# Expert routing computed from the unnormalised residual

## The reference

```python
xl = xl + g1_l[:, None] * yl
hl2 = modulate(rms_norm(xl, norm_ffn[i]), sh2_l, sc2_l)
xl = xl + g2_l[:, None] * expert_choice_ffn(hl2, router[i], w_gate[i], w_up[i], w_down[i])

def rms_norm(x, g):      # modulate(h, shift, scale) = h * (1 + scale) + shift
    return x * rsqrt(mean(x * x, axis=-1) + EPS) * g

def expert_choice_ffn(h, router, w_gate, w_up, w_down):
    cap = 2 * n // 16                       # 32 tokens for each of 16 experts
    aff = softmax(h @ router, axis=-1)
    gate, idx = top_k(aff.transpose(0, 2, 1), cap)
    xg = h[bidx, idx]
    hid = silu(xg @ w_gate) * (xg @ w_up)
    y = (hid @ w_down) * gate[..., None]
    return zeros_like(h).at[bidx, idx].add(y)
```

## Time and profile before

| | us |
|---|---|
| median of 3 runs (lowest, highest) | 1381.2 (1380.23, 1385.59) |
| profiled execution, its span | 1381.7 |
| TensorE busy | 1168.3 (85%) |
| VectorE busy | 625.0 (45%) |
| ScalarE busy | 432.9 (31%) |
| DMA | 338.65 MB, 245 GB/s mean |
| experts of layer 0: first gate matmul to last down chunk | 387.2 to 597.8 |
| experts of layer 1 | 737.5 to 937.5 |

### The profile page before, as it was taken

How to read it: one execution, slowest core, us unless ns; L and a number is a source line. 1 busy time by engine, 2 the same in 40 slices (tenths; PEclk the granted TensorE clock), 3 DMA queues, 4 the chain that set the end, 5 groups by cost and what they waited for, 6 DMA issues and landing times.

```text
span 1381.7 us, 19453 instructions
## 1 busy us (share of the span) xinstructions
PE 1168.3 (85%) x8209; PEld 864.1 (63%) x8209; DVE 625.0 (45%) x1142; ACT 432.9 (31%) x783; POOL 77.9 (6%) x118
## 2 busy tenths in 40 slices
PE   5999979999986656689999665668999999999887
PEld 2777758876832212159994221216999778899766
DVE  3655874555520101146753011015994555545574
ACT  2546523312300000044341000003545663443552
POOL 3000224430000000000000000000000000100000
PEclk9999999999998889899999898989999989999998
DMA  9745964238689999985759999997354213355000
GB/s 330 288 160 206 325 224 139 106 130 307 244 316 409 409 409 409 409 316 183 305 215 377 409 409 410 409 409 284 123 183 140 105 55 129 122 183 184 0 1 31
DMA packets 125099, 338.65 MB, mean 245 GB/s; under 512 B 8657, under 2 KB 11590, under 8 KB 125014
## 3 DMA queue, kind: packets, MB, share of 16 engines
q1 hardware_dynamic: 117536, 334.51, 63.7%
q10 hardware_dynamic: 7478, 2.91, 0.8%
HBM read 336.35 MB, written 1.05 MB: 244 GB/s over the span
## 4 chain that ended last, share of the span: by engine, by line
PE 61%; DMA 26%; DVE 8%; ACT 2%; SPq 2%; issue 1%; ACTq 0%; DVEq 0%
PE bank L684 9%; PE bank L686 9%; PE bank L685 9%; DMA arena<-in_w_up_dram 6%; DMA expert_slots<-in_w_gate_dram 5%; DMA weight_ring<-in_w_up_dram 4%; DMA weight_ring<-in_w_gate_dram 3%; DMA expert_slots<-in_w_down_dram 3%; PE bank L971 3%; PE bank L586 3%; DVE arena L1902 3%; PE bank L1144 2%; PE bank L816 2%; PE bank L663 2%; PE bank L664 2%; DMA weight_ring<-in_ada_w_dram 2%
## 5 line engine op out<-in xcount | busy, mean ns | idle before, releaser
L684 PE MATMUL bank<-input_high,weights_high 128*128 128x256 f32 (+1 forms) x992 | 290.5, 293 | 8.2 <-DVE input_low L1902 7.5
L686 PE MATMUL bank<-input_high,weights_low 128*128 128x256 f32 (+1 forms) x992 | 283.9, 286 | 0.0
L685 PE MATMUL bank<-input_low,weights_high 128*128 128x256 f32 (+1 forms) x992 | 283.8, 286 | 0.0
L1902 DVE TENSOR_TENSOR weights_low<-weight_ring,weights_high 128x1024 fp32r<-128x1024 f32 x142 | 173.6, 1224 | 165.5 <-ACT weights_high L1439 165.2
L684 PEld LDWEIGHTS bank<-input_high,weights_high 128*128 128x128 f32 x992 | 188.3, 190 | 13.7 <-issue 10.6
L1439 ACT ACTIVATE weights_high<-weight_ring 128x1024 fp32r<-128x1024 f32 x142 | 149.6, 1055 | 143.5 <-PE bank L686 143.1
L686 PEld LDWEIGHTS bank<-input_high,weights_low 128*128 128x128 f32 x992 | 188.5, 190 | 0.0
L685 PEld LDWEIGHTS bank<-input_low,weights_high 128*128 128x128 f32 x992 | 187.9, 189 | 0.7
L1902 DVE TENSOR_TENSOR arena<-arena,bank 128x512 f32<-128x512 f32 (+1 forms) x38 | 24.6, 651 | 261.2 <-PE bank L971 240.2
L971 PE MATMUL bank<-arena 128*32 128x512 f32 x384 | 61.2, 773 | 50.0 <-DMA arena<-in_w_up_dram 38.8
L971 PEld LDWEIGHTS bank<-arena 128*32 128x32 f32 x384 | 12.3, 129 | 96.7 <-DMA arena<-in_w_up_dram 43.5
(11 more groups left out here) (414 smaller groups left out, 1748.2 us busy)
## 6 DMA issues: line engine op xcount, KB each, us to landing
weight_ring<-in_ada_w_dram SPq DMA_DIRECT2D x24, 2048.0 KB, 9.4
weight_ring<-in_w_gate_dram SPq DMA_DIRECT2D x16, 2048.0 KB, 23.6
arena<-in_w_up_dram SPq DMA_DIRECT2D x16, 2048.0 KB, 24.2
weight_ring<-in_w_down_dram SPq DMA_DIRECT2D x16, 2048.0 KB, 24.0
arena<-in_w_down_dram SPq DMA_DIRECT2D x12, 2048.0 KB, 20.3
weight_ring<-in_even_w_in_dram SPq DMA_DIRECT2D x9, 2048.0 KB, 8.6
arena<-in_w_gate_dram SPq DMA_DIRECT2D x8, 2048.0 KB, 21.4
weight_ring<-in_w_up_dram SPq DMA_DIRECT2D x8, 2048.0 KB, 16.2
```

The lines of the kernel that those rows point to most:

```text
L684: pe.matmul(b[:, 0:width], hi[:, k, :], XHI[:, k, t0:t0 + width], start=k == 0, stop=False)
L685: pe.matmul(b[:, 0:width], hi[:, k, :], XLO[:, k, t0:t0 + width], start=False, stop=False)
L686: mm = pe.matmul(b[:, 0:width], lo[:, k, :], XHI[:, k, t0:t0 + width], start=False, stop=k == KD - 1)
L1902: return dve.tensor_tensor(out_, a, b, op)
```

## The change

**The routing** takes the residual as it is. For a token x with root r the logit is r * (x . (gain * router)) + shift . router, where gain = (1 + scale) * norm weight. `router_gains` (VectorE) makes `GS` (gain and shift) and `RTG` = router times gain; `route_prepare` (TensorE) sums shift . router, the same on all partitions (`BROW`), and turns `GS`. `route_behind` puts into the output product, behind quarter 0, four tiny matmuls that bring gain and shift into the order of the gathered features (`GPERM`); behind quarter 4, eight transposes of residual tiles; behind quarter 7, six more, then the products of seven tiles with `RTG` in four column groups (`LPART`), two more transposes, and the logits. ScalarE (`route`, `token_rows`) squares each transposed piece from PSUM with an accumulator and copies it to `H2`; so each token's sum of squares is on its own partition, and the root is taken of 128x2 numbers. ScalarE scales `H2` by the root beside the selection. Gain and shift are applied when the gathered tokens leave PSUM.

**The selection** reads its bank without a copy; the mask is turned apart from the running count and multiplied behind the transpose; `PT` is made first for four experts, then for twelve. The gather drains in four quarters. The norms over features of `norm(1, ...)` and `norm(3, ...)` are gone, and `h2T` is no longer written there.

**The slots** are filled in another order, and slots 8 and 9 wait for the product's input to be split instead of for the token transposes. The small DMAs of ScalarE are issued behind the scaling of `H2`. The diff, cut:

```diff
-FILL_ORDER = (4, 5, 0, 1, 2, 3, 6, 7, 8, 9)
+FILL_ORDER = (4, 5, 0, 1, 8, 9, 2, 3, 6, 7)
...
-            warm(8)
-            pe.wait_ge(vector_drained, n["v"])
...
+            def route_prepare(ly):
+
+                pe.wait_ge(route_prep, ly + 1)
+                b = v_open()
+                for k in range(KD):
+                    pe.matmul(b[:, 0:16], GS[:, 8 + k:9 + k].broadcast_to([P, P]), RT[:, k, :], start=k == 0, stop=k == KD - 1)
+                v_close(pe.transpose(b[0:16, P:2 * P], GS, ident[:, :]), ("route", ly))
...
+                    if m == 4:
+                        tokens(0, 4)
+                    if m == KD - 1:
+                        tokens(4, 3)
+                        b = v_open()
+                        for k in range(KD - 1):
+                            j = 32 * (k % 4)
+                            mm = pe.matmul(b[j:j + 32, 0:T], RTG[:, 16 * k:16 * k + 32], XH[:, k, META:L2], start=k < 4, stop=k >= 3)
+                        parts = v_close(mm, ("parts", ly))
+                        pe.wait_ge(vector_drained, mark[(name, KD - 1)])
+                        b = s_open()
+                        mm = transposes(b, [(b[:, tt * P:tt * P + P], XH[:, KD - 1, META + tt * P:META + tt * P + P]) for tt in range(TT)])
+                        s_close(mm, ("last_rows", ly))
...
+            pe.wait_ge(vector_drained, n["v"])
+            route_prepare(0)
+            warm(4)
             for j in range(2):
-                product(W_EVO + j, 4 * j, T, v_open, v_close, "out1", new_input=j == 0, after=norm_behind(1, T, SQn))
+                product(W_EVO + j, 4 * j, T, v_open, v_close, "out1", new_input=j == 0, after=route_behind(0, "out1"))
...
-                warm(9)
-                pe.wait_ge(router_in, 16 * (ly + 1))
...
-                turn_tokens(0)
+                warm(4)
                 pe.wait_ge(aff_ready, ly + 1)
...
-                turn_tokens(1)
-                warm(4)
+                warm(6)
+                pe.wait_ge(mask_ready, ly + 1)
...
-                warm(2)
-                pe.wait_ge(pick_ready, 2 * ly + 1)
-                pe.wait_ge(scalar_drained, n["s"])
+                warm(1)
+                pe.wait_ge(pick_ready, 3 * ly + 1)
+                pe.wait_ge(tokens_scaled, 4 * (ly + 1))
...
                 if slot_of(cn) >= LATE_SLOT:
-                    sp.wait_ge(scalar_filled, mark[("h2", stream[cn][1])])
+                    sp.wait_ge(input_split, KD * (1 + 2 * stream[cn][1]))
...
+            def token_rows(ly, tt, k0, count):
+
+                b = take()
+                act.activation(SQJ[:, 0:count * P], b[:, 0:count * P], ACT.Square,
+                               accum_out=tok_sum[:, k0 // 4, tt:tt + 1]).then_inc(token_squares, 1)
+                drained(act.activation(H2[:, tt, k0 * P:(k0 + count) * P], b[:, 0:count * P], ACT.Copy))
+                act.wait_ge(scalar_drained, n["s"])
...
             def experts(ly):
                 act.wait_ge(sm_args, ly + 1)
                 act.activation(AFFT, AFFT, ACT.Exp).then_inc(sm_exps, 1)
+                act.wait_ge(scalar_drained, n["s"])
+                act.wait_ge(token_rstd, ly + 1)
+                for tt in range(TT):
+                    for kh in range(2):
+                        h = H2[:, tt, 512 * kh:512 * kh + 512]
+                        act.activation(h, h, ACT.Copy, scale=tok_rstd[:, tt:tt + 1]).then_inc(tokens_scaled, 1)
...
-            norm(1, ("out1",), mod=(0, 24))
+            route(0)
...
+            def router_gains(ly):
+
+                dve.wait_ge(router_in, 16 * (ly + 1))
+                then(stt(GS[:, 0:8], MOD[:, ly, 32:40, 0], 1.0, vec("norm_ffn", 8 * ly, 8), ADD, MUL))
+                then(dve.tensor_copy(GS[:, 8:16], MOD[:, ly, 24:32, 0]))
+                tt(RTG.rearrange("p (k e) -> p k e", k=KD), RT, last(GS[:, 0:8], 16), MUL).then_inc(route_prep, 1)
...
-                drained(dve.tensor_copy(AT2[0:EXP, :], b[0:EXP, 0:T]), True)
...
-                tt(PS2[0:EXP, :], PS2[0:EXP, :], MT2[0:EXP, :], MUL).then_inc(pos_ready, 1)
-                b = take()
-                drained(dve.tensor_copy(POS, bank(b, 2, 16)), True)
+                b = take()
+                dve.wait_ge(scalar_drained, mark[("maskT", ly)])
+                drained(tt(POS, bank(b, 2, 16), MASKT, MUL), True)
...
-                for t_, pt in enumerate(pts):
-                    ins = tt(pt, last(POS[:, t_, :], CAP), mid(SLOTN, EXP), ALU.is_equal)
-                ins.then_inc(pick_ready, 1)
+                for e0, e1 in ((0, EG), (EG, EXP)):
+                    for t_, pt in enumerate(pts):
+                        ins = tt(pt[:, e0:e1, :], last(POS[:, t_, e0:e1], CAP), mid(SLOTN, e1 - e0), ALU.is_equal)
+                    ins.then_inc(pick_ready, 1)
```

More of the change, by code:

```diff
@@ L928, in experts @@
                 v_close(mm, ("affT", ly))
-                turn_tokens(1)
-                warm(4)
+                warm(6)
+                pe.wait_ge(mask_ready, ly + 1)
+                b = s_open()
+                for tt in range(TT):
+                    mm = pe.transpose(b[:, 16 * tt:16 * tt + 16], MT2[0:EXP, tt * P:tt * P + P], ident[0:EXP, 0:EXP])
+                s_close(mm, ("maskT", ly))
                 pe.wait_ge(pos_ready, ly + 1)
@@ L966, in experts @@
                             w = weights(cn + q, "p (e k n) -> p e k n", e=EG, k=2)
-                            if part == 0 and q == 2:
-                                pe.wait_ge(vector_drained, gathered)
+                            if part == 0:
+                                pe.wait_ge(*gathered[q])
                             for k in range(2):
@@ L1034, in _ @@
             product(W_SC + 5, 4, T, v_open, v_close, "gb")
-            warm(8)
+            route_prepare(1)
+            warm(4)
             for j in range(2):
-                product(W_SC + 6 + j, 4 * j, T, v_open, v_close, "out2", new_input=j == 0, after=norm_behind(3, T, SQn))
+                product(W_SC + 6 + j, 4 * j, T, v_open, v_close, "out2", new_input=j == 0, after=route_behind(1, "out2"))
             mark[("split", 1)] = len(quarters)
@@ L1670, in _, with route @@
                     drained(act.activation(OT[:, :, u * P:u * P + P], bank(b, 4, P), ACT.Copy))
+            def token_rows(ly, tt, k0, count):
[4 more added lines that the diff above has]
+                act.wait_ge(scalar_drained, n["s"])
+            def route(ly):
+                for m in range(KD):
+                    high()
+                    if m == 5:
+                        for tt in range(TT):
+                            token_rows(ly, tt, 0, 4)
+                for tt in range(TT):
+                    token_rows(ly, tt, 4, 3)
+                b = take()
+                for tt in range(TT):
+                    act.activation(SQJ[:, tt * P:tt * P + P], b[:, tt * P:tt * P + P], ACT.Square,
+                                   accum_out=tok_sum[:, 2, tt:tt + 1]).then_inc(token_squares, 1)
+                act.wait_ge(token_sums, ly + 1)
+                then(act.activation(tok_rstd, tok_part, ACT.Ln, bias=EPSC, scale=1.0 / D))
+                act.activation(tok_rstd, tok_rstd, ACT.Exp, scale=-0.5).then_inc(token_seed, 1)
+                drained(act.activation(H2[:, :, (KD - 1) * P:KD * P], bank(b, 2, P), ACT.Copy))
             def experts(ly):
@@ L1711, in _ @@
                 high()
-            norm(3, ("out2",), mod=(1, 24))
+            route(1)
             n["segment"] += 1
@@ L2221, in _ @@
                         split()
+                        router_gains(0)
                     dve.wait_ge(o_rstd, a - 1)
@@ L2283, in experts @@
                 for g in range(GROUPS):
-                    b = take()
-                    drained(dve.tensor_copy(XG[:, 4:8], bank(b, 4, P)))
+                    for k0 in (2, 6):
+                        b = take()
+                        for k in range(2):
+                            ins = dve.tensor_scalar(XG[:, k0 + k, :], b[:, k * P:k * P + P], GPERM[:, 0, k0 + k:k0 + k + 1],
+                                                    GPERM[:, 1, k0 + k:k0 + k + 1], MUL, ADD)
+                        drained(ins)
                     b = take()
```

148 lines of the change are left out of this document (107 added, 41 removed).

## The result

The changed kernel takes 1376.5 us (median of 5 runs, 1375.6 to 1378.7) where the kernel before, run beside it, takes 1385.6 (5 runs): ratio 0.993, 95% interval 0.990 to 0.996. That is faster, by 0.7%; 1366 was forecast, with 1372 as the upper end. The profiled execution has a span of 1374.6 and a time of 1376.5.

The account below looks back on a forecast made before the run. Each expert layer was taken as bound by the chunk stream, counted from chunk 10's landing. Gains of 9.5 (layer 0) and 5.9 (layer 1) took the span from 1381.7 to 1366.3, forecast time 1366 us, range 1359.5 to 1372.

Parts of the forecast that it names:

- The shorter routing: Between output product and gather: exponential at End + 6.0 instead of 10.0, gather at End + 14.2 instead of 19.2 us.
- End: End of the last matmul of the output product before the experts; in layer 0 forecast 0.5 us later.
- Rival 2: Routing and gather: gather at 1.2 GHz and mask late; layer 1 gains 0.9, layer 0 7.5 us; 1373 us, chance 0.12.
- The product and P: Layer 0's output product starts (P) at 340.0 instead of 338.2 and ends 0.5 us later; layer 1's ends 1.0 earlier.
- One line for both queues: Layer 0 loads: small DMAs wait for bulk issued before them, and the next bulk chunk waits behind them, some 10 us.
- Chunk 10: First chunk of a layer to reuse a slot; in layer 0 to land at 397.4 instead of 406.9, gain 9.5 us.
- Rival 1: Layer 0 loads: small DMAs share the stream from their issue; chunk 10 lands at 393.2, gain 13.7; 1361 us, chance 0.20.
- The hole: Layer 0 stream behind chunk 9: some 10 us in which only ScalarE's short packets move.
- The order of slots: Expert loads: chunks 4 and 5 go to slots 8 and 9 early, so all ten are issued before the small DMAs.
- The sum: Whole kernel: layer 0 gains 9.5 and layer 1 5.9, together 15.4 us; span 1381.7 to 1366.3, chance 0.52.

Follow-up runs that it names:

- before_fourth: The kernel before, unedited, in a later profiled execution; time 1392.2 us, span 1390.2.
- prep_early: The changed kernel with layer 0's routing preparation ahead of the wait for the last bank, between two warm-ups of 4; 1372.6 us.
- small_early: The changed kernel with layer 0's five small DMAs issued by ScalarE before the output product; 1373.4 us, ratio to the kernel before 0.990.
- both_early: The changed kernel with the edits of small_early and prep_early together; 1368.7 us, ratio to the kernel before 0.988.
- old_slots: The changed kernel with the slot fill order of the kernel before; 1381.6 us.
- both_warm: both_early plus warm-ups before each layer's last down chunk (6), the scan (6 for 3) and the scores (8); 1361.5 us, ratio to the kernel before 0.981.

## Why the prediction was wrong, step by step

**The shorter routing** was right. Exponential at End + 5.4 (6.0), gather at End + 12.8 (14.2). Rival 2 was half of it: at 1.2 GHz in its first part the gather took 5.57 in layer 0 and 5.34 in layer 1, where 0.5 a layer was in the sum, so End to the first gate matmul came out at 18.3, as reckoned (14.2 + 4.0). Layer 1 won 6.2 for 5.9 (7.2 against before_fourth).

**The product and P** was mis-sized. The reckoning had P at 340.0, with the preparation and the warm-up at full clock; they stood behind an idle wait of 2.6 us and ran mostly at the 1.2 GHz level, 3.16 + 3.83 for 1.9 + 1.8 reckoned, and P was 342.3, End 2.7 later than forecast. prep_early gave 3.8 of it back.

**One line for both queues** was wrong as worded, and its number right. Small DMAs don't wait for bulk in front of them: in the earlier trace rows no short packet runs until 377 because their DMAs had only been issued from 374.0 on, which I read as waiting. In six profiles, with and without the change, the first short packet follows the first issue by 3 to 4 us, in the midst of bulk (small_early: issue at 335.0, first packets after 338, while the bulk runs on at some 400 GB/s). In the changed kernel they ran beside the bulk (322 and 338 GB/s above). What does wait is bulk issued behind them. Chunk 10 was issued at 387.5 and landed 12.4 us later. The 8.7 that I had for a landing without short packets, counted from the use of chunk 0, was too long as well: in small_early it is 7.8 from the issue, in both_early 7.4, which is why small_early won 5.0 and not 3.6. Since the first chunk behind the small DMAs bears the wait in either reading, the forecast of 397.4, moved by the 2.7 of End, gives 400.1 for a measured 399.8: luck, as far as the mechanism goes. Rival 1, sharing from the issue on, was right on the mechanism for bulk already issued and wrong on chunk 10. The hole that I foretold, some 10 us of short packets only, was in good part a stream without work, as small_early shows.

**The order of slots** had its gain put down to layer 0. old_slots shows that it also carries 2.6 of layer 1's 6.2, and that the small DMAs' cost depends on it.

**The sum** failed in the step from the layers to the end. Forecast span 1366.3, measured 1374.6. Of the 8.3, layer 0 gave 7.1 instead of 9.5 at its last chunk (2.4, from End), layer 1 0.3 more, and tail, scan and scores took 6.0; that makes 8.1. These three were not in the sum at all: I took the profiled execution's stages for constants, and it was a short one. The step from span to time added 2.4: the time lies 1.9 above the span of its own execution (1376.5 and 1374.6), while I had set the median of three runs, 0.5 below the span of another execution, against it.

The range was too narrow for the same reason: it held rivals inside the layers only, none for unchanged stages that the clock lengthens by up to 9 us from one execution to the next (123.5 to 132.6 for the three in five profiles of the kernel before), which the three times shown (1380.2 to 1385.6) hinted at. The like-for-like saving of 15.6 us, so close to the 15.4 of the sum, is partly luck: before_fourth's P was itself late by 1.4 against the first profile, and its layer 1 a microsecond longer.

## What to carry to other kernels

Before you subtract from a profiled span, ask whether that execution is a usual one: compare its unchanged stages across two or three profiles, and put the spread of those stages into the range. Issue DMAs of short runs where the next bulk transfer is far off, never just ahead of one that the critical path waits for; here 10 us of a layer hung on four of them. And fill idle or narrow TensorE stretches with full-width work only where the next stage is bound by TensorE.

## What the hardware showed that I had not expected

The granted clock fell to 1.2 GHz with TensorE busy all the time: 19.0 of 19.0 us, clock 0.55, in the scan's narrow matmuls; with one full-width matmul per step, 1.8 us in all, it stayed at 1.00 in both kernels that have it, and the scan was 2.7 to 2.8 us shorter than in both_warm. That the narrowness of the other matmuls is what lets it fall is the likeliest reading; no run separates it from other properties of that work. Small DMAs of 20 KB, and 64 KB for the router, held two chunks of 2 MB for nearly nine microseconds when issued ahead of them. Issued behind the bulk they alternated with it packet by packet and cost from almost nothing (1.19 MB in 3 us) to about a fifth of its rate (321 GB/s instead of 409 over 20 us). And unchanged stages 200 to 570 us behind an edit can move by more than the edit itself: with the gather of layer 1 delayed by 6.4 us, tail, scan and scores together were 9.8 shorter in the profiled execution. The kernel before has the same spread without any edit, so the delay need not be the cause.
